# Recurrence of a hybrid encoder layer: the square, its product and the growth moved within the written order of the engines

## The reference

```python
def step(state, inp):
    r_t, w_t, k_t, v_t, an_t, b_t = inp
    sa = jnp.einsum('bhij,bhj->bhi', state, an_t)
    state = (state * w_t[:, :, None, :] + sa[..., None] * b_t[:, :, None, :]
             + v_t[..., None] * k_t[:, :, None, :])
    return state, jnp.einsum('bhij,bhj->bhi', state, r_t)
```

## Time and profile before

| | |
|---|---|
| median of 3 runs | 4709.09 us |
| the profiled execution | 4716.15 us, its span 4714.4 us |
| PE, DVE, ACT, POOL busy over the span | 88%, 62%, 47%, 25% |
| first `x12` of the recurrence, its last matmuls | 1713.67 us, 2740.20 us |
| from 1736 to 2716 us | PE 809.92 us busy of 980, DVE 448.66, ACT 363.33 |

### The profile page before, as it was taken

How to read it: one execution, slowest core, us unless ns; L and a number is a source line. 1 busy time by engine, 2 the same in 40 slices (tenths; PEclk the granted TensorE clock), 3 DMA queues, 4 the chain that set the end, 5 groups by cost and what they waited for, 6 DMA issues and landing times. The chain is left out here.

```text
span 4714.4 us, 123717 instructions
## 1 busy us (share of the span) xinstructions
PE 4143.5 (88%) x50861; PEld 3797.6 (81%) x50862; DVE 2915.9 (62%) x5152; ACT 2228.8 (47%) x4176; POOL 1175.0 (25%) x954
## 2 busy tenths in 40 slices
PE   6979999975999968888888869944999999999998
PEld 5869999965888856667676747734999999999998
DVE  5879999965888854444444447756444444444443
ACT  4568888854666633333333322201444444444443
POOL 4544444421344420110102223301112112112111
PEclk9989999998999979999999979966999999999999
DMA  8920000014444332222222246603556556556554
GB/s 167 187 61 26 22 23 26 23 32 136 144 153 143 127 133 67 66 66 64 67 64 67 60 124 203 196 25 95 168 175 180 170 172 184 168 171 184 170 172 108
DMA packets 555357, 540.74 MB, mean 115 GB/s; under 512 B 80320, under 2 KB 502464, under 8 KB 554944
## 3 DMA queue, kind: packets, MB, share of 16 engines
q1 hardware_dynamic: 489920, 435.44, 29.6%
q10 hardware_dynamic: 50240, 52.44, 4.9%
q0 software_dynamic: 14784, 46.57, 4.8%
HBM read 377.92 MB, written 156.43 MB: 113 GB/s over the span
## 5 line engine op out<-in xcount | busy, mean ns | idle before, releaser
L2298 DVE TENSOR_TENSOR g_wlo<-g_raw,g_whi 128x2048 fp32r<-128x2048 f32 x192 | 439.1, 2287 | 115.3 <-ACT g_whi L2260 115.3
L2260 ACT ACTIVATE g_whi<-g_raw 128x2048 fp32r<-128x2048 f32 x192 | 366.4, 1908 | 145.0 <-DMA g_raw<-expert_w_gate 145.0
L2369 PE MATMUL g_pD<-g_whi,g_hh 128*128 128x256 f32 x1536 | 417.3, 285 | 2.5 <-ACT g_o L2287 2.4
L2369 PE MATMUL g_pD<-g_wlo,g_hh 128*128 128x256 f32 x1536 | 408.1, 279 | 0.0
L1119 PE MATMUL c_pP<-c_xh,c_whi 128*128 128x258 f32 x1120 | 328.6, 293 | 34.7 <-DMA c_gup<-g_lora_up 29.3
L587 DVE TENSOR_TENSOR sapl<-sapT,saph 128x512 fp32r<-128x512 f32 x512 | 329.9, 686 | 2.7 <-ACT saph L546 2.7
L577 DVE TENSOR_REDUCE sanm<-sapS 128x1 f32<-128x1024 f32 x256 | 313.5, 1225 | 25.8 <-PE sapS L628 15.8
L2231 POOL DMA_INDIRECT g_x<-hn_rows,index x48 | 69.4, 1446 | 1035.2 <-PE g_pU L2353 1024.9
L546 ACT ACTIVATE saph<-sapT 128x512 fp32r<-128x512 f32 x512 | 278.8, 596 | 94.1 <-PE sapT L640 94.0
L1344 POOL TENSOR_TENSOR d_kr<-d_kr,d_fixed 128x512 f32<-128x512 f32 x80 | 101.8, 1273 | 880.0 <-ACT d_kr L1370 880.0
L1119 PE MATMUL c_pP<-c_xh,c_wlo 128*128 128x258 f32 x1120 | 319.9, 286 | 0.0
(11 more groups left out here) (369 smaller groups left out, 12445.8 us busy)
## 6 DMA issues: line engine op xcount, KB each, us to landing
g_raw<-expert_w_gate SPq DMA_DIRECT2D x64, 1024.0 KB, 5.0
g_raw<-expert_w_up SPq DMA_DIRECT2D x64, 1024.0 KB, 8.3
g_raw<-expert_w_down SPq DMA_DIRECT2D x64, 1024.0 KB, 5.0
ops<-c_ops SPq DMA_DIRECT2D x40, 1024.0 KB, 4.2
d_bd<-ops SPq DMA_DIRECT2D x160, 256.0 KB, 3.1
c_xh<-xT_hi SPq DMA_DIRECT2D x10, 1032.0 KB, 5.8
c_xl<-xT_lo SPq DMA_DIRECT2D x10, 1032.0 KB, 9.2
x_in<-x SPq DMA_DIRECT2D x20, 512.0 KB, 8.2
```

The lines of the kernel that those rows point to most:

```text
L2260: act.activation(w_hi[:, Q % NBUF, :, :], raw[:, Q % NRAW, :, :], ACT.Copy).then_inc(s["g_hi"], 1)
L2298: dve.tensor_tensor(w_lo[:, Q % NBUF, :, :], raw[:, Q % NRAW, :, :], w_hi[:, Q % NBUF, :, :].bitcast(F32), ALU.subtract).then_inc(s["g_lo" ...
L2369: mm = pe.matmul(pD[k][:, 0:WB], x[:, d, k * P:(k + 1) * P], w[:, b, d, :], start=(d == 0 and i == 0), stop=(d == DC - 1 and i == len(part ...
```

## The change

Four functions of the order move. `squared` and `smallest` of a chunk go from part 1 of the slot of its `x12` to part 0 of the next slot. `fours`, on PE and on ACT, goes from part 0 to part 1 of that slot. `grown`, on PE and on DVE, goes from the end of part 1 to its front, ahead of the side work of its own group. No instruction is added or removed, no wait is changed, and SP and POOL are untouched. PE's order becomes:

```diff
@@ ACT, run @@
                 if part == 0:
-                    if l == 0 and is_chunk(m):
-                        fours(m, par, g)
                     if l > 0 and is_chunk(m):
                         stationary(m, par, l - 1, g)
 ...
                 else:
+                    if l == 0 and is_chunk(m):
+                        fours(m, par, g)
@@ DVE, run @@
                 if part == 0:
+                    if l == 0 and is_chunk(m):
+                        smallest(m, g)
                     if 0 < l <= NL and is_chunk(m):
                         between(m, l - 1, g)
 ...
                 else:
+                    if 0 < l <= NL and is_chunk(m):
+                        grown(m, par, l - 1, g)
                     if l == 0 and is_chunk(m - 1):
                         through(m - 1, g)
 ...
-                    if 0 < l <= NL and is_chunk(m):
-                        grown(m, par, l - 1, g)
-                    if l == STEPS - 1 and is_chunk(m + 1):
-                        smallest(m + 1, g)
             reads(0, 0, 0)
-            smallest(0, 0)
@@ PE, run @@
                 if part == 0:
                     if l == 0 and is_chunk(m):
-                        fours(m, g)
+                        squared(m, g)
 ...
                 else:
+                    if l == 0 and is_chunk(m):
+                        fours(m, g)
+                    if 0 < l <= NL and is_chunk(m):
+                        grown(m, par, l - 1, g)
                     if l == 0 and is_chunk(m - 1):
                         through(m - 1, 1 - par, g)
 ...
-                    if 0 < l <= NL and is_chunk(m):
-                        grown(m, par, l - 1, g)
-                    if l == STEPS - 1 and is_chunk(m + 1):
-                        squared(m + 1, g)
             x12(0, 0, 0)
-            squared(0, 0)
```

## The result

The changed kernel took 4766.43 us (median of 8 runs, 4749.74 to 4798.92), the kernel before 4716.19 us beside it (8 runs, 4705.29 to 4741.99). The ratio is 1.0107, 95% interval [1.0078, 1.0136]: slower by 50 us. The forecast was 4699 us, with a range up to 4745. The profiled execution of the changed kernel is the longest of its eight, 4798.92 us, so the two traces lie further apart than the medians. Windows of both traces say where. Of each kernel, the first row is all that stands ahead of the recurrence and the second the recurrence, with the columns of the earlier trace rows.

A forecast was written before the change was run, and what follows sets the result against it. No engine full; PE leads and loses 170 us to waits in the recurrence. Stops 3.63 against 3.61 us a cycle, restarts winning 0.3 x 39 x 0.88 = 10 us: 4699 us, range 4660 to 4745.

The forecast's parts named there:

- The new stops: PE's stops after the change, gathered into four or five: 3.63 us a cycle against 3.61 before.
- 1.70 us ahead of `between` g0: Slot 2 into 3: PE stands still for DVE's `yo` where `squared` and stops of 0.60 and 0.49 were.
- 1.08 ahead of `grown` g1: Slot 5: new PE stop of 1.08 us, `grown` waiting for DVE's `pm` and ACT's `Y`.
- `x12`'s 0.47: PE's `x12` waiting for `turned`'s copies once a cycle: existing 0.22 us plus 0.25 from `grown` moved ahead.
- `zs` 0.33: PE's stop for DVE's `zs`, claimed to stay at 0.33 us because its distance from `through` is kept.
- The other signs that were to show the forecast right: PE waits for `fewT` ahead of `squared` and `d_z` ahead of transposes near 0; full-clock cycle about 23.2 us.
- The restarts: PE saves 0.18 us per block following without a stop; three fewer stops taken as 0.3 us a cycle, 10 us.
- the prediction's own rival: PE's longer stops bring the lower clock in every cycle, a fall of some 7 us: 4766 us; chance 0.15.
- The price of 0.43 us for each us at the lower level: Recurrence: cost of PE's lower clock level, about 50 us in all for 118 us there.
- Issue: PE's waits of kind issue, 26.1 us in the largest group, held to be removable by no order.
- `fours` or POOL: `fours` keeps enough distance and POOL's mask waits for unmoved `kr`: cost nothing; `fours` without cover 0.4 us a time.
- `turned`'s 0.25 us: Slot 4: `grown` of the same group ahead of `turned` delays `x12` by 0.2 to 0.4 us, taken as 0.25.

The follow-up runs named there:

- e1: Kernel before with only `grown` moved to the front of part 1 on PE and DVE; 4740.4 us against 4716.7, ratio 1.0027.
- e16: Changed kernel plus five idle matmuls a cycle on PE ahead of `between` g0 in slot 3; 4750.5 us against 4719.4 before, ratio 1.0052.
- e17: e12 plus five idle matmuls a cycle on PE ahead of `between` g0 in slot 3; 4702.4 us against 4719.4 before, ratio 0.9960.
- e18: e2 plus five idle matmuls a cycle on PE ahead of `between` g0 in slot 3; 4724.2 us against 4719.4 before, ratio 1.0017.
- e12: Changed kernel with loads cut to 8 of 128 partitions and `state` without its `tv` product; 4726.4 us against 4719.4 before, ratio 0.9998.
- e9: Changed kernel with `state` lacking its product with `tv` (less code and work); 4722.1 us against 4713.5 before, ratio 1.0019.
- e10: Kernel before with `state` lacking its product with `tv` (less code and work); 4695.2 us against 4713.5, ratio 0.9952.
- e3: Changed kernel plus idle PE matmuls, five ahead of `between` g0 and three ahead of `grown` g1; 4796.2 us against 4716.7 before, ratio 1.0142.
- e6: Kernel before with loads of chunks 2 to 39 cut to 8 of 128 partitions; 4675.2 us against 4723.6, ratio 0.9896.
- e2: Kernel before with only `squared`, `smallest` and `fours` moved half a slot later; 4749.8 us against 4716.7, ratio 1.0061.
- e11: Kernel before with each chunk's loads of keys and values issued in three parts; 4702.8 us against 4713.5, ratio 0.9973.

## Why the prediction was wrong

**The new stops** were read rightly: 1.70 us ahead of `between` g0 measured 1.65 to 1.79 in 29 of 37 halves and 1.1 to 1.5 in the others, 1.08 ahead of `grown` g1 1.18, `x12`'s 0.47 measured 0.43, `zs` 0.33 measured 0.23. Missed were 0.20 for `yo` ahead of `between` g1 and 0.16 for `pm`. The fastest halves hold 3.9 us of stops (0.43 + 1.18 + 0.20 + 0.16 + 1.68 + 0.23) where those of before hold 3.7.

The other signs that were to show the forecast right came as well (`fewT` and `d_z` near 0, cycles of 23.0 us at full clock), and the one that was to show it wrong, a mean clock under 0.90, stood at 0.90. They spoke of undisturbed cycles alone, and these were forecast well; the time went elsewhere.

**The restarts** are the step of the sum that failed first. Three stops fewer were to give back 0.3 us a cycle. Outside its stops, PE takes 22.73 - 3.67 = 19.06 us in the fastest cycle before and 23.01 - 3.88 = 19.13 after: they give nothing. The 0.18 us that a block seemed to save without a stop ahead of it was read from one place. The sum of the order is thus up to +0.3 us a cycle, 4 to 11 us lost instead of 10 won. e1 shows the same from the other side: its fastest halves hold 2.3 us of stops, 1.4 less than before, and its cycle is only 0.35 us shorter. PE is busy 19.7 us in them instead of 19.1, with the same 672 matmuls. Why is open; the profile models the ends of matmuls.

**The clock** was the larger error, and the prediction's own rival, at 0.15. The price of 0.43 us for each us at the lower level was right, the pair of half cycles gives 0.41. The place was right too, the stretch with the stop of 1.70 us and 2.3 us busy of 4, measured at 2.25. What I took as evidence against it, that stops elsewhere go, did not count. The rival's 4766 us is the measured number, but not by its working: it had 155 us more at the lower level, a fall of 7 us in every cycle, and there were 52 us more (171 against 119), most falls 3.4 us long and behind a third of the stops. By these 52 x 0.41 = 21 us. Of the 52, 34 lie behind the stop for `yo` (48 against 14), the other 18 behind issue stalls. By e16, e17 and e18, which take the falls behind `yo` away, it is 16 to 26 (18 to 26 by the ratios). A fall cost less in other traces, 0.8 us in e12, so 21 is an upper value. The Trainium skill (TensorE: Matmul & The Clock Gate, "A second HAM failure mode: psum-queue depth-cycling") has PE's short idling between groups of matmuls as what makes the clock swing. The runs agree, and add that the total of idling was not what counted here: 3.7 and 3.9 us of stops in a cycle, but in eight pieces or with one of 1.75.

**Issue** was set aside as what "no order of the work removes". That is where the prediction had no term at all, and the changed order adds 19 us of it (68 against 49), `grown` alone 20 (e1). Where PE's short stops are gone, it goes through its instructions in dense runs, and in the row 1966.20:1969.60 above it went through 146 matmuls and as many weight loads, 292 instructions in 3.4 us, where a block holds 257 and the next one starts 3.5 us later at the closest, 4.8 in the middle. That the dense runs outpace the blocks fits the traces, and e9 and e10 fit it, but it was not shown by an experiment that changed it alone. Part of the falls of the clock go with it too: of all those in the 75 half cycles, 12 of 21 had 0.4 us or more of issue stalls in the 4.5 us ahead of them before and 22 of 34 after.

The sum for the two profiled recurrences: 11 for the order, 21 for the clock, 19 for issue, 51 of the 57 us, with the first two at their upper values. What was shown by switching it off and on is the clock behind the stop for `yo`; the other parts are read from single traces. No part was found that rests on `fours` or POOL, which the prediction had at nothing; the loads matter only in that short ones shorten the issue stalls of either order. `turned`'s 0.25 us came out as 0.21 (0.43 against 0.22).

**Open**: what issue alone costs; when the chip asks for the next block (ahead of the longest stall the two blocks before were 6.0 us apart while the DMA engines had idle time), why the same stop brings a fall in 12 cases of 37 and not in the others, and why e1's shorter stops don't shorten its cycle by as much.

## What to carry to other kernels

Waits gathered into one long stop are not worth the same as short ones spread out: look in the windows at the granted clock right behind the longest stop, price a fall from a pair of equal stretches with and without it, and fill the stop with idle matmuls to test it. Before costing removed waits as gains, subtract the undisturbed stretches of two orders from each other: here 102 us of waits went and none of it was won. Stalls of kind issue followed the landings of the instruction blocks here, so in a kernel of small matmuls count them, and the falls of the clock behind them, before making PE's work denser: an order can lose there what it saves in waits. That the blocks' rate is the cause was argued, not shown.

## What the runs showed of the hardware

- In the recurrence PE's instructions come in 16 KB blocks on a DMA queue of their own; this is its row from 1740 to 2720 us of the changed kernel:

```profile
q8 instruction: 193, 3.16, 1.4%
```

- Taking 2496 PE instructions out of the recurrence (e9) took 9 of its 214 blocks away, and 1280 more (e3) added 5.
- In each of the 20 traces 97% or more of the issue stalls there (32 to 107 of them) ended 1.15 to 1.65 us after such a landing. A random moment lies there in 10 to 11% of cases.
- Data loads in the background cost this: with loads cut to 8 of 128 partitions, issue stalls fell from 49 to 34 us and the kernel before by 48 us (e6).
- In the 75 half cycles the falls of the clock last 3.4, 6.8 or 10.2 us, and one 13.7 us (e1); a fall of 3.4 us costs 0.8 to 1.4 us of time (12.1 against 10.7 in the changed kernel, 11.9 against 10.5 in e2, 11.8 against 11.0 in e12).
- Five idle 128x128 matmuls a cycle cost less than the falls that they prevent: 16 us gained in e16, 26 in e18.
- Of the kernels that do the whole computation only e11 came out under the one before, with 0.9973 [0.9948, 0.9998], hardly told from 1.
